# Triangular inverses in blocks of 32 instead of 64 in two recurrent stages

## The reference

```python
def rwkv_step(S, inp):
    r_t, w_t, k_t, v_t, kk_t, a_t = inp
    sa = jnp.einsum('dbhij,dbhj->dbhi', S, -kk_t)
    S = (S * w_t[..., None, :] + sa[..., :, None] * (kk_t * a_t)[..., None, :]
         + v_t[..., :, None] * k_t[..., None, :])
    y = jnp.einsum('dbhij,dbhj->dbhi', S, r_t)
    return S, y
...
        # gdn_chunk_scan
        sol = lax.linalg.triangular_solve(eye - a, rhs, left_side=True, lower=True, unit_diagonal=True)
```

## Time and profile before

| | |
|---|---|
| median of 3 runs | 2194.05 us (2193.01 to 2203.64) |
| profiled execution, its own time | 2197.27 us |
| its span | 2195.2 us |
| TensorE busy in the span | 2009.1 us (92%), 14924 matmul records |
| VectorE | 1090.6 us (50%) |
| ScalarE | 667.1 us (30%) |
| GpSimd | 398.2 us (18%) |
| the masks of the inverse, L767 | 336 instructions, 257.1 us |
| first stage with inverses (`stage_core`) | about 242 to 597 us of the span |
| second (`stage_recur`) | about 1480 to 1752 us of the span |

### The profile page before, as it was taken

The page is one execution under the profiler, slowest core; times in us unless marked ns, Lnnn a source line. Parts: engine busy times, 40 slices in busy tenths (PEclk is TensorE's granted clock), DMA queues, the critical chain, the costliest instruction groups (busy, mean ns, idle before and its releaser), DMA issues. The chain is left out here.

```text
span 2195.2 us, 36198 instructions
## 1 busy us (share of the span) xinstructions
PE 2009.1 (92%) x14924; PEld 1540.9 (70%) x14924; DVE 1090.6 (50%) x1818; ACT 667.1 (30%) x1191; POOL 398.2 (18%) x485
## 2 busy tenths in 40 slices
PE   6999889998999968978799999998888899999997
PEld 4776677787878853322477877567788777888886
DVE  6565455455376851101267653466766675332333
ACT  4555333332233222211246432103111133312321
POOL 1000275655200001111000000005435201100100
PEclk9999999899999989999899999999999999999999
DMA  5221000000066679999732122240000042333331
GB/s 193 81 81 65 29 2 2 2 2 2 31 237 232 222 271 372 412 413 410 315 142 67 58 68 93 86 154 2 2 2 2 20 174 68 96 98 94 96 96 48
DMA packets 73960, 265.66 MB, mean 121 GB/s; under 512 B 10966, under 2 KB 11478, under 8 KB 72784
## 3 DMA queue, kind: packets, MB, share of 16 engines
q1 hardware_dynamic: 60848, 225.94, 28.5%
q10 hardware_dynamic: 7488, 25.95, 3.4%
q0 software_dynamic: 5472, 11.59, 1.4%
HBM read 254.82 MB, written 17.30 MB: 124 GB/s over the span
## 5 line engine op out<-in xcount | busy, mean ns | idle before, releaser
L207 DVE TENSOR_TENSOR weights_lo<-ring,weights_hi 128x1024 fp32r<-128x1024 f32 x162 | 200.3, 1237 | 175.9 <-ACT weights_hi L203 175.9
L203 ACT CAST weights_hi<-ring 128x1024 fp32r<-128x1024 f32 x162 | 169.1, 1045 | 296.2 <-PE ps L226 277.3
L767 POOL TENSOR_TENSOR gdn_M<-xT,const 64x256 f32<-64x256 f32 x144 | 107.7, 748 | 417.7 <-DVE xT L3307 384.5
L225 PE MATMUL ps<-wide_b_round,weights_hi 128*128 128x512 f32 (+1 forms) x448 | 165.8, 370 | 0.0
L232 PE MATMUL ps<-const 128*128 128x128 f32 x1028 | 146.7, 294 | 4.8 <-PEq L2905 2.4
L224 PE MATMUL ps<-wide_a_round,weights_hi 128*128 128x512 f32 x344 | 144.2, 419 | 4.0 <-DVE wide_b_round L647 3.7
L232 PEld LDWEIGHTS ps<-const 128*128 128x128 f32 x1028 | 131.7, 203 | 11.1 <-issue 7.5
L226 PE MATMUL ps<-wide_a_round,weights_lo 128*128 128x512 f32 x344 | 136.8, 398 | 0.0
L224 PE MATMUL ps<-wide_b_round,weights_hi 128*128 128x512 f32 (+1 forms) x360 | 131.1, 364 | 2.0 <-DVE wide_a_round L3698 2.0
L226 PE MATMUL ps<-wide_b_round,weights_lo 128*128 128x512 f32 (+1 forms) x360 | 130.3, 362 | 0.0
L224 PE MATMUL ps<-mlp_hi,weights_hi 128*128 128x512 f32 x320 | 125.7, 393 | 4.1 <-DVE mlp_lo L3648 4.1
(11 more groups left out here) (593 smaller groups left out, 4048.3 us busy)
## 6 DMA issues: line engine op xcount, KB each, us to landing
ring<-stream_in SPq DMA_DIRECT2D x210, 512.0 KB, 3.6
moe_ring<-stream_in SPq DMA_DIRECT2D x112, 512.0 KB, 15.0
w_mod<-w_mod_in ACTq DMA_DIRECT2D x40, 512.0 KB, 5.1
wide_b<-stream_in SPq DMA_DIRECT2D x32, 512.0 KB, 14.1
xT<-w_mod_in SPq DMA_DIRECT2D x16, 512.0 KB, 4.1
na_rel<-rel_in POOLq DMA_DIRECT2D x4, 640.0 KB, 5.9
mod_acc<-mod_part ACTq DMA_DIRECT2D x5, 512.0 KB, 6.0
ring<-mod_acc SPq DMA_DIRECT2D x1, 2560.0 KB, 18.6
```

The source lines that it names most:

```text
L203: act.copy(self.hi[:, i % self.n, :], w).then_inc(self.cast.sem, self.cast.up())
L207: eng.tensor_tensor(self.lo[:, i % self.n, :], self.unit(i)[0], self.hi[:, i % self.n, :], ALU.subtract).then_inc(self.k.used, 1)
L225: pe.matmul(out, left[0], right[1], start=False, stop=False, **kw)
L767: ins = pool.tensor_tensor(self.M[half, lv % 2, hs, :], lt[half, :, half], m, ALU.mult)
```

## The change

Each triangle is cut into four diagonal blocks of 32x32, which lie on the four quarters of the partitions. Levels 0 to 4 run on those, on four tiles of the array. The copies `T` of the diagonal blocks are cut out once by GpSimd (`take`, four instructions a group), and one `mask` of 128x128 then serves all four quarters. Level 5, which joins two blocks of 32 to one of 64, is done as one 32x32 block beside the diagonal: `pe_last_y` and `pe_last_z` take the corner of the triangle directly, on two tiles, and `last` writes the negative of z into `whole`, the 64x64 inverses. GpSimd's `place` copies the diagonal inverses into `whole` (four instructions a task); `whole` is zeroed once by `clear`. `first_half` and `second_half` read `whole`, with one more wait. There is no mask of level 5 any more. The tables in `const` shrink.

```diff
-    def mask(self, pool, n, lv, g, lt, lower):
...
-        a = CONST["lv64_b" if lower else "lv64_f"][0] + lv * 64
-        for half in (slice(0, 64), slice(64, P)):
-            m = k.const[half, a:a + 64].unsqueeze(1).broadcast_to([64, 4, 64])
-            ins = pool.tensor_tensor(self.M[half, lv % 2, hs, :], lt[half, :, half], m, ALU.mult)
-        ins.then_inc(self.masked.sem, self.masked.up())
+    def take(self, pool, n, g, lt):
+        if g:
+            pool.wait_ge(self.masked.sem, self.masked.at(10 * n + 1))
+        elif n:
+            pool.wait_ge(self.masked.sem, self.masked.at(10 * n))
+            pool.wait_ge(self.placed.sem, self.placed.at(n))
+        else:
+            pool.wait_ge(self.zeroed.sem, self.zeroed.at(1))
+        for q in QUARTERS:
+            ins = pool.tensor_copy(self.T[q, 4 * g:4 * g + 4, :], lt[q, :, q])
+        ins.then_inc(self.cut.sem, self.cut.up())
+
+    def mask(self, pool, n, lv, g, lower):
...
+        a = CONST["lv32_b" if lower else "lv32_f"][0] + lv * 32
+        m = k.const[:, a:a + 32].unsqueeze(1).broadcast_to([P, 4, 32])
+        pool.tensor_tensor(self.M[:, (5 * n + lv) % 2, hs, :], self.T[:, hs, :], m, ALU.mult).then_inc(self.masked.sem, self.masked.up())
+
+    def place(self, pool, n):
+        pool.wait_ge(self.zeroed.sem, self.zeroed.at(1))
+        pool.wait_ge(self.flipped.sem, self.flipped.at(8 * n + 8))
+        for q in QUARTERS:
+            ins = pool.tensor_copy(self.whole[q, n % 2, :, within(q)], self.XT[q, :, :])
+        ins.then_inc(self.placed.sem, self.placed.up())
 
     def quads(self, pe, out, left, right):
         for h in range(4):
-            for half in (slice(0, 64), slice(64, P)):
-                mm = pe.matmul(out(h, half), left(h, half), right(h, half), start=True, stop=True)
+            for q in QUARTERS:
+                mm = pe.matmul(out(h, q), left(h, q), right(h, q), start=True, stop=True)
         return mm
...
+    def pe_last_y(self, pe, n, g, lt, lower):
+        k = self.k
+        pe.wait_ge(self.updated.sem, self.updated.at(10 * n + 6 + g + 1))
+        for h in range(4):
+            for a, b in corners(lower):
+                cols = slice(b.start, b.stop)
+                mm = pe.matmul(k.ps[b, self.bank + g, h * 32:(h + 1) * 32], lt[a, h, cols], self.X[a, 4 * g + h, :], start=True, stop=True)
+        mm.then_inc(self.y_ready.sem, self.y_ready.up())
...
     def copy_y(self, act, n, lv, g):
         act.wait_ge(self.y_ready.sem, self.y_ready.at(10 * n + 2 * (lv - 1) + g + 1))
-        act.copy(self.Y[:, 4 * g:4 * g + 4, :], self.k.ps[:, self.bank + g, 0:256].rearrange("p (h t) -> p h t", t=64)).then_inc(
+        act.copy(self.Y[:, 4 * g:4 * g + 4, :], self.k.ps[:, self.bank + g, 0:P].rearrange("p (h t) -> p h t", t=32)).then_inc(
             self.y_copied.sem, self.y_copied.up())
...
+    def last(self, dve, n, g, lower):
+        k = self.k
+        dve.wait_ge(self.zeroed.sem, self.zeroed.at(1))
+        dve.wait_ge(self.z_ready.sem, self.z_ready.at(10 * n + 8 + g + 1))
+        for a, b in corners(lower):
+            ins = dve.tensor_scalar(self.whole[a, n % 2, 4 * g:4 * g + 4, within(b)],
+                                    k.ps[a, self.bank + 2 + g, 0:P].rearrange("p (h t) -> p h t", t=32), -1.0, None, ALU.mult)
+        ins.then_inc(self.updated.sem, self.updated.up())
...
                     pe.wait_ge(inv.updated.sem, inv.updated.at(10 * i + 10))
+                    pe.wait_ge(inv.placed.sem, inv.placed.at(i + 1))
                     for h in range(RH):
-                        mm = pe.matmul(k.ps[F, 6, h * HD:(h + 1) * HD], inv.XT[F, i % 2, h, :], w_sb[F, h % 2, h // 2, :], start=True, stop=True)
+                        mm = pe.matmul(k.ps[F, 6, h * HD:(h + 1) * HD], inv.whole[F, i % 2, h, :], w_sb[F, h % 2, h // 2, :], start=True, stop=True)
```

More of the change, by code:

```diff
@@ L740, in halves_of, with corners, within @@
     return (slice(0, 64), slice(64, P)) if d == "f" else (slice(64, P), slice(0, 64))
+QUARTERS = [slice(32 * q, 32 * q + 32) for q in range(4)]
+def corners(lower):
+    return [(QUARTERS[q + lower], QUARTERS[q + 1 - lower]) for q in (0, 2)]
+def within(q):
+    return slice(q.start % 64, q.start % 64 + 32)
 class Inverse:
@@ L815, in dve_first @@
[L815 to L818, removed]
-        dve.transpose(X.rearrange("p h t -> p (h t)"), XT.rearrange("p h t -> p (h t)")).then_inc(
+        k, hs = self.k, slice(4 * g, 4 * g + 4)
+        eye = k.c("eye32").unsqueeze(1).broadcast_to([P, 4, 32])
@@ L976, in second_half @@
                     for h in range(RH):
-                        mm = pe.matmul(k.ps[G, 6, h * HD:(h + 1) * HD], inv.XT[G, i % 2, h, :], w_sb[G, h % 2, h // 2, :], start=True, stop=True)
+                        mm = pe.matmul(k.ps[G, 6, h * HD:(h + 1) * HD], inv.whole[G, i % 2, h, :], w_sb[G, h % 2, h // 2, :], start=True, stop=True)
                     mm.then_inc(u2_ready.sem, u2_ready.up())
@@ L1018, in _ @@
                     C, S, R = t < N, 1 <= t <= N, t >= 2
+                    lower = int(S and TASKS[t - 1][0] == "b")
                     if R:
@@ L1029, in _ @@
                             keep_busy(k, pe, 3 if lv == 2 else 8, 6)
-                        if S:
+                        if S and lv < FAST - 1:
                             inv.pe_y(pe, t - 1, lv, 0)
                             inv.pe_y(pe, t - 1, lv, 1)
+                        elif S:
+                            for g in range(2):
+                                inv.pe_last_y(pe, t - 1, g, As[(t - 1) % 2][:, 4 * g:4 * g + 4, 0:P], lower)
                         if R and lv == 1:
@@ L1233, in _ @@
                             mask(t, 2 * lv - 7)
-                        if S:
+                        if S and lv < FAST - 1:
                             inv.update(dve, t - 1, lv, 0)
                             inv.update(dve, t - 1, lv, 1)
-                            if lv < FAST - 1:
-                                inv.flip(dve, t - 1, lv, 0)
-                                inv.flip(dve, t - 1, lv, 1)
+                            inv.flip(dve, t - 1, lv, 0)
+                            inv.flip(dve, t - 1, lv, 1)
+                        elif S:
+                            inv.last(dve, t - 1, 0, lower)
+                            inv.last(dve, t - 1, 1, lower)
                         if C and lv < 3:
@@ L1277, in _ @@
                     for lv in range(1, FAST):
-                        if S:
+                        if S and lv < FAST - 1:
                             for g in range(2):
-                                inv.mask(pool, t - 1, lv, g, lt(t - 1, g), lower)
+                                inv.mask(pool, t - 1, lv, g, lower)
+                        elif S:
+                            inv.place(pool, t - 1)
                         if C and lv < 3:
@@ L2993, in first_half @@
                         for h in range(4):
-                            mm = pe.matmul(of_heads(i, 6, F)[:, h, :], inv.XT[F, n % 2, 4 * i + h, :], W[F, i, h, :], start=True, stop=True)
+                            mm = pe.matmul(of_heads(i, 6, F)[:, h, :], inv.whole[F, n % 2, 4 * i + h, :], W[F, i, h, :], start=True, stop=True)
                     mm.then_inc(u1_ready.sem, u1_ready.up())
@@ L3009, in second_half @@
                         for h in range(4):
-                            mm = pe.matmul(of_heads(i, 6, other)[:, h, :], inv.XT[other, n % 2, 4 * i + h, :], W[other, i, h, :], start=True, stop=True)
+                            mm = pe.matmul(of_heads(i, 6, other)[:, h, :], inv.whole[other, n % 2, 4 * i + h, :], W[other, i, h, :], start=True, stop=True)
                     mm.then_inc(u_ready.sem, u_ready.up())
@@ L3457, in _ @@
                             pool.wait_ge(lt_done.sem, lt_done.at(2 * t + g + 1))
-                            inv.mask(pool, t, 0, g, lt(t, g), g == 1)
+                            inv.take(pool, t, g, lt(t, g))
+                            inv.mask(pool, t, 0, g, g == 1)
         k.stage_end()
```

99 lines of the change are left out of this document (61 added, 38 removed).

## The result

Over 20 executions each, the kernel before takes 2203.78 us (2193.01 to 2215.19) and the changed kernel 2190.53 us (2158.20 to 2199.62). Over all 20 of each, the medians are 13 us apart and the means 17. The direction was right, the size came out between a third and a bit over half of that, and the median is just above the range of 2136 to 2188.

What follows compares the result with a forecast made beforehand. TensorE's in-order queue, with VectorE chains let in at a few places, was taken as the bound. First stage -26.5, second -27.8, borders +7, clock +5 gave -42: 2152 us against the median 2194.05, range 2136 to 2188.

Steps and rivals of the forecast that it cites:

- clock term: Cost for TensorE idling more: two more stretches at the lower clock, 2.5 us each, +5 us.
- Rival A: Four tiles don't give four times the pace, 0.015 us a record, bursts stay 0.9 us: 2167 us; chance 0.21.
- C: Rival: engine starts one record per 0.020 us, bursts 1.3 us, about -8 us: 2186 us; chance 0.08.
- D: Rival: 0.030 us a record is the engine's own limit, bursts 1.9 us, about +54: 2248 us; chance 0.05.
- (a): First stage, middle iteration, y1 through y2 up to L989: z1 and y2 bursts shorten, -0.6 us, borders charged separately.
- (b): First stage, middle iteration, z2 to second tokens transpose (L910): shorter VectorE chain without GpSimd's level-5 mask beside it, -1.9 us.
- (c): First stage, middle iteration, z3, then L923 and its mask: -0.4 us, set by ScalarE and VectorE.
- (d): First stage, middle iteration, y4, z4, y5 beside VectorE masks of L923, whose 2.5 us period stays: gain 0.
- (e): First stage, middle iteration, z5 with half the columns: 0.5 us less, of which the last mask leaves 0.35.
- The iteration with bare bursts: First stage's eighth, a bare chain of four levels (burst, copy, burst, update), each giving about 0.7: -3.5 us.
- rival B: Bursts no longer fill the score part; eight more lower-clock stretches give 20 us back: 2172 us; chance 0.12.
- Rival E: GpSimd's chain of cuts and placement sets the end, parts over 1 us each, nothing gained: 2194 us; chance 0.02.

Runs made afterwards that it cites:

- full fillers: Changed kernel plus independent 128x128 `keep_busy` matmuls ahead of TensorE's waits in both stages: 2154.20 us, ratio 0.9766; repeated, 2153.67 us, ratio 0.9754.
- one-tile run: Changed kernel with full fillers, each burst reordered so one array tile works at a time: 2314.42 us, a single execution.
- fillers of its own: Kernel before with extra `keep_busy` matmuls at the same places in both stages, fewer where it idled less: 2197.17 us, ratio 0.9952.

## Why the forecast was right in its parts and wrong in its size

The step that failed is the clock term of the costs: +5 was charged, and it came to 20 to 23 us (its paragraph is below). At equal clock the change is worth 42 to 43 us, and the sum without its clock term was -26.5 - 27.8 + 7 = -47. By its steps:

**Pace.** 0.009 us a record was taken, 0.0086 measured. That is luck: a tile is held 0.021 us, not 0.033 (weights and moving side both went from 64 to 32 columns, and no run parts them), and four tiles side by side give 2.4 times the pace of one, not four times. The two errors cancel. Rival A's premise, that four tiles don't give four times the pace, is so for these records, but not its 0.015 us; C and D fall. The Trainium skill ("TensorE: Matmul & The Clock Gate", section "Wait — 56ns, not 53.3ns?") has no two starts closer than about 25 ns. The trace disagrees: 8.6 ns over four array tiles. On one tile at a time it was 20.6 ns, below the page's figure too. The 33 us that the prediction draws from that figure don't follow from its own rivals: between C (0.020 us, -8) and D (0.030, +54) the page's 0.025 comes to about +23.

**First stage, middle iteration: -2.75 with its borders forecast, -2.55 measured** in the one iteration without a lower stretch (-1.9 to -2.8 in the five with full fillers). (a) To z2 it is 21.03 us instead of 20.81, where -0.1 was forecast; 0.57 of it is a stall of the issue kind at 432.2. Without it -0.35, so the borders between tile shapes cost some 0.25 us there and not 0.5 (an estimate; no run changes them alone). At y1's the next shape starts 0.14 us after the burst's last start, 428.99 behind 428.85. (b) z2 to the second tokens transpose 3.44 us instead of 5.66: -2.2 for -1.9. (c) On to the first scores 1.33 for 1.66: -0.3 for -0.4. (d) The scores come every 2.53 us as before, with 0.71 idle instead of 0.31: 0, as forecast. (e) From the last scores to L942 4.12 for 4.35: -0.2 for -0.35.

**First stage, its ends.** The first iteration with inverses takes 29.32 us instead of 35.73, which had 6.8 us at the lower clock; without the clock some -3, as forecast. The iteration with bare bursts was mis-sized. Before, TensorE in the ninth, in order of time:

```profile
571.52 1.15 PE L773 MATMUL ps<-rw_X,rw_M 64*64 64x64 f32 x32
572.67 1.15 PE L773 MATMUL ps<-rw_Y,rw_XT 64*64 64x64 f32 x32
573.96 1.15 PE L773 MATMUL ps<-rw_X,rw_M 64*64 64x64 f32 x32
```

The bursts already followed each other every 1.15 to 1.29 us: the other group's matmuls cover one group's copy and update. Shorter bursts uncover that path. In the changed kernel y3 starts 1.14 us after z2 instead of 1.29, and z3 0.84 after y3 instead of 1.15: 0.15 and 0.31 gained, where 0.4 of burst and at the updates 0.26 of VectorE were counted. With three steps of each kind about -1.4, not -3.5 (whose own working, four levels of 0.7, gives -2.8). The fillers cost there as well: z2 to z5 takes 7.32 us before and 10.34 with full fillers, 0.66 of it stalls, which is why a held clock isn't free.

**Second stage: -4.6 a middle iteration forecast, -3.4 measured** (43.95, 43.73 and 45.37 us before; 40.48, 40.40 and 41.94 with full fillers at the full clock; without fillers none of them kept it). Of the 1.2 us that are missing, most is z5 with the step ahead of it. The wait ahead of `gla_decays` was 0.41 us for VectorE and is, with fillers,

```profile
1579.85 1.16 PE L3113 MATMUL ps<-const,gla_la 128*128 128x128 f32 x8 [1.23 <-DVE xT L3406]
```

so 0.8 of the gain became a longer wait for the VectorE product that was late next. I had cut TensorE's share there without asking what VectorE does meanwhile. The rest isn't traced, and the fillers may have a part in it.

**A term that was missing: instruction supply.** 6.3 us of issue idle, none before. -47 + 6 is within 2 us of the -42 to -43, but that isn't a closed account. The ninth iteration fell 2 us short and the second stage's three middle ones 3.6, which would leave -35; the smaller borders give some of that back, and part of the idle time may stand where it costs nothing. No row of before could show it as a stall. The Trainium skill ("Runtime: NRT & Kernel Launch", section "Instruction fetch mechanics") gives blocks of 16 KiB, 256 instructions, and says that their fetch is mostly hidden, by the sequencer's own pace. The trace agrees with the block (16384 bytes, about 126 records with as many weight loads) and not with the rest: with records at 0.0086 us, TensorE stood still 8 times for 0.2 to 1.3 us.

**The clock: the step that failed.** "TensorE idle more, I charge two more stretches at 2.5 = +5". Two stretches of 5 us were charged; the profiled execution has 99 us more at the lower clock in the two stages, and over the executions the cost is 20 to 23 us. The price was off the other way: half of such a stretch was taken as lost, and the slopes of the two lines give 0.33 to 0.38 us for each us at the lower clock. The forecast saw the 0.8 us waits ahead of the scores coming, listed them as a sign that (d) was right, and gave rival B, "bursts no longer fill the score part", 0.12 and 20 us. Its 20 us were right, and its mechanism in kind: fillers in the waits take the stretches away. What it missed is their form and place: not eight short stretches behind score parts but, for the most part, three long ones (23.9, 27.3, 30.7 us), only the first of them out of a score part, in which the clock stayed low although TensorE was busy for 21.31 of 22.00 us. I argued that lower stretches come after work that the change doesn't touch; in the first stage those stayed at 3.4 to 6.8 us, and the new ones came elsewhere. Idle time is what the fillers took away with them; that it is the whole cause isn't shown, as the one-tile run and the six score parts without a long stretch say.

**GpSimd.** Masks 0.463, cuts 0.286, placements 0.392 us an operation, where 0.44, 0.44 and 0.7 were taken; in the first stage its busy time fell from 185.29 to 100.90 us, more than the 60 forecast. No idle time of TensorE ends with the placement. Rival E falls.

## What to carry to other kernels

Taking work off TensorE in gaps that another engine bounds buys nothing there and can cost elsewhere: ask for each new idle gap what it may do to the clock, and price the chance of a long stretch at half speed, not only the gap. Compare kernels at equal mean clock, or with the gaps filled, before concluding that a change saved less than its sum; here the change is worth 24 us bare; with some 190 extra matmuls in its waits the changed kernel stands 52 to 54 us under the bare kernel before, and 43 under that kernel with fillers of its own. And where two groups take turns, a shorter burst helps only down to the other group's copy and update.

## What the runs showed of the hardware

A 32x32 fp32 record with 32 moving columns holds its tile for 20.6 ns; two tiles give one per 11.4 ns, four one per 8.6. TensorE can outrun its instructions: with four-tile bursts at that pace it stood still for 0.2 to 1.8 us at a time, 8 to 14 times in the two stages, and each time went on 2.2 to 2.9 us after a 16 KB instruction transfer had begun; two transfers were never closer than 3.3 us. The changed kernel's executions spread over 41 us (2158 to 2200) along a line of 1650 us per unit of mean clock, with 1.7 us of scatter. A 128x512 VectorE product that starts beside a 64x256 GpSimd product takes 1.21 to 1.22 us instead of 0.68; one begun 0.24 us ahead of it is not slowed.
